# One core, a two-layer decoder trunk: the front of the recurrent layer with scaled evictions, six banks of low-rank products, and memory attention interleaved with the value strips

## The reference, cut to what matters

```python
proj = hn @ rwkv_w_in[j]
prev = jnp.pad(proj, ((0, 0), (1, 0), (0, 0)))[:, :-1]
xs = proj + (prev - proj) * mu                     # token shift
w = -jax.nn.softplus(-(w0 + jnp.tanh(wl) @ w2)) - 0.5
a = jax.nn.sigmoid(a0 + al @ a2)
g = jax.nn.sigmoid(gl) @ g2
kk = (k * k_k); kk = kk * rsqrt(max(sum(kk * kk), 1e-24))   # per head
k = k * (1.0 + (a - 1.0) * k_a)
bonus = sum(r * k * r_k) * v                       # per head
...
s = einsum('bshd,bmhd->bhsm', q, mem_k) * HEAD_DIM ** -0.5
p = softmax(s); mo = einsum('bhsm,bmhd->bshd', p, mem_v)
mix = concatenate([prim, mo]) @ w_out[i]
```

## Time and profile before

| | |
|---|---|
| median of 3 runs | 791.8 us (790.52 to 792.34) |
| the profiled execution's own time | 790.41 us |
| its span, first to last instruction | 788.7 us, mean granted clock 0.974 |
| PE busy | 736.8 us (93%) |
| DVE / ACT / POOL busy | 489.3 (62%) / 405.6 (51%) / 97.8 us (12%) |
| front of layer 1, first turned strip to first chunk matmul | 382.6 to 483.5 us |

### The profile page before, as it was taken

How to read it: one execution, slowest core, us unless ns; L and a number is a source line. 1 busy time by engine, 2 the same in 40 slices (tenths; PEclk the granted TensorE clock), 3 DMA queues, 4 the chain that set the end, 5 groups by cost and what they waited for, 6 DMA issues and landing times.

```text
span 788.7 us, 15563 instructions
## 1 busy us (share of the span) xinstructions
PE 736.8 (93%) x6725; PEld 641.1 (81%) x6725; DVE 489.3 (62%) x707; ACT 405.6 (51%) x641; POOL 97.8 (12%) x148
## 2 busy tenths in 40 slices
PE   3999998999999999999798788999899999999996
PEld 3879966788888888888787677999888888888885
DVE  4787776647766656444776995333557766566522
ACT  6654766548554555335865423333237645555311
POOL 4020076500000000000701004700000000000000
PEclk9999989999999999999979898999999999999998
DMA  8846710036565655565713430000026656565511
GB/s 299 298 143 207 256 46 1 2 114 229 166 198 175 198 176 197 180 209 161 227 53 111 158 106 3 4 5 4 3 82 223 203 165 207 164 211 166 209 54 54
DMA packets 78278, 111.73 MB, mean 142 GB/s; under 512 B 2124, under 2 KB 64738, under 8 KB 78210
## 3 DMA queue, kind: packets, MB, share of 16 engines
q1 hardware_dynamic: 77090, 107.67, 41.4%
q0 software_dynamic: 976, 3.04, 1.2%
q10 hardware_dynamic: 144, 0.04, 0.0%
HBM read 109.68 MB, written 1.05 MB: 140 GB/s over the span
## 4 chain that ended last, share of the span: by engine, by line
PE 77%; DVE 13%; ACT 6%; issue 2%; DMA 1%; POOL 1%; SPq 0%; DVEq 0%; ACTq 0%; POOLq 0%
PE ps L968 19%; PE ps L681 10%; PE ps L1109 10%; PE ps L682 10%; PE ps L683 10%; PE ps L970 10%; DVE w_lo L1706 3%; ACT w_hi L1276 2%; PE ps L813 2%; PE ps L839 2%; PE ps L790 1%; DVE x_hi_lo L1926 1%; DMA w_raw<-w_mem_kv 1%; DVE row_max L1786 1%; ACT scores L1342 1%
## 5 line engine op out<-in xcount | busy, mean ns | idle before, releaser
L1706 DVE TENSOR_TENSOR w_lo<-w_raw,w_hi 128x2048 fp32r<-128x2048 f32 (+2 forms) x101 | 227.4, 2263 | 91.4 <-ACT w_hi L1276 91.3
L968 PE MATMUL ps<-x_hi_lo,w_hi 128*128 128x512 f32 x640 | 226.5, 399 | 0.0
L1276 ACT ACTIVATE w_hi<-w_raw 128x2048 fp32r<-128x2048 f32 (+2 forms) x101 | 189.1, 1890 | 43.7 <-PE ps L683 42.9
L970 PE MATMUL ps<-x_hi_lo,w_lo 128*128 128x256 f32 x640 | 179.8, 281 | 0.0
L968 PEld LDWEIGHTS ps<-x_hi_lo,w_hi 128*128 128x128 f32 x640 | 120.3, 188 | 29.9
L970 PEld LDWEIGHTS ps<-x_hi_lo,w_lo 128*128 128x128 f32 x640 | 120.9, 189 | 0.0
L681 PE MATMUL ps<-w_hi,x_hi_lo 128*128 128x512 f32 (+3 forms) x240 | 82.7, 345 | 3.5 <-DVE x_hi_lo L1926 3.0
L683 PE MATMUL ps<-w_hi,x_hi_lo 128*128 128x512 f32 (+3 forms) x240 | 81.0, 337 | 0.0
L682 PE MATMUL ps<-w_lo,x_hi_lo 128*128 128x512 f32 (+3 forms) x240 | 81.0, 337 | 0.0
L681 PE MATMUL ps<-w_hi,hidden_hi 128*128 128x512 f32 x176 | 68.6, 390 | 0.0
L682 PE MATMUL ps<-w_lo,hidden_hi 128*128 128x512 f32 x176 | 68.5, 389 | 0.0
(11 more groups left out here) (365 smaller groups left out, 1122.5 us busy)
## 6 DMA issues: line engine op xcount, KB each, us to landing
w_raw<-w_ffn_in SPq DMA_DIRECT2D x44, 1024.0 KB, 5.1
w_raw<-w_ffn_out SPq DMA_DIRECT2D x22, 1024.0 KB, 4.9
w_raw<-rwkv_w_in SPq DMA_DIRECT2D x11, 1024.0 KB, 5.5
w_raw<-w_out SPq DMA_DIRECT2D x8, 1024.0 KB, 5.1
w_raw<-nsa_w_in SPq DMA_DIRECT2D x6, 1024.0 KB, 14.7
w_raw<-w_mem_kv SPq DMA_DIRECT2D x2, 1024.0 KB, 8.5
w_raw<-nsa_cmp_k_w SPq DMA_DIRECT2D x2, 1024.0 KB, 5.6
w_raw<-nsa_cmp_v_w SPq DMA_DIRECT2D x2, 1024.0 KB, 5.6
```

Source lines behind the costliest of these rows:

```text
L968: pe.matmul(psum[:, bank + j, :], kt_of(w_hi, i, k)[:, c], xx[:, k, :, :].rearrange("p c n -> p (c n)"), start=k == 0, stop=False)
L970: ins = pe.matmul(psum[:, bank + j, 0:SEQ], kt_of(w_lo, i, k)[:, c], xh[:, k, :], start=False, stop=k == KD - 1)
L1276: act.activation(w_hi[:, i % SPL, 0:size(i)], raw[:, i % RAW, 0:size(i)], ACT.Copy).then_inc(hi_done, 1)
L1706: dve.tensor_tensor(w_lo[:, i % RAW, 0:size(i)], raw[:, i % RAW, 0:size(i)], w_hi[:, i % SPL, 0:size(i)], ALU.subtract).then_inc(lo_done, 1)
```

## The change

The **token shift** becomes two evictions and one sum. ACT writes mu * strip into `shift_in` and (1 - mu) * strip straight into the destination, in four instructions of 128x256 with a per-partition scale where one copy of 128x512 stood; DVE adds the two in one instruction. The column 1 - mu (and 1 - k_a) is made once in `cols_m` by two small DVE instructions in layer 0. The **low-rank products** use six banks (0, 1, 2 for z and 3, 6, 7 for a), so that no pair waits for an eviction; PE no longer waits for the gate's sigmoid ahead of them, strip 3 comes ahead of the gate products, and ACT takes all three z before the three a and the gate's sigmoid after them. The factor 1 + (a - 1) * k_a goes from DVE to ACT, and the squares of `kk` from POOL to ACT. The **memory query** strip moves ahead of the value strips (`MQ` = 7), and the steps of the memory attention are put between and inside the strips 8, 9 and 10 (`feature_strip` gets a `between` after its first half), with the maxima, exponentials and copies put between the splits and strips of ACT and DVE. The turned probabilities go to bank 6, all values to bank 7, from which one ACT and one DVE instruction make the high and low part; only the last chunk waits for them. The products with exp(sums) move from q = 6 to q = 7 on DVE.

```diff
-RWKV_ORDER = [9, 3, 4, 5, 0, 1, 2, 6, 7, 8, 10]
+RWKV_ORDER = [9, 3, 4, 5, 0, 1, 2, 10, 6, 7, 8]
+MQ = RWKV_ORDER.index(10)
...
+        colM = put("one_minus_mu_ka", [P, 26])
...
-        pT1 = at(o_x, "probsT_1", [P, 2, 2, 2, P])
+        pT1 = at(o_cs, "probsT_1", [P, 2, 2, 2, P])
...
+        def strip_dst(q):
+            f0 = 2 * RWKV_ORDER[q]
+            dst = wg if q == 0 else (rT, k_T, vT)[f0 // FT]
+            j0 = 0 if q == 0 else f0 % FT
+            return f0, [dst[:, j0 + i, :] for i in range(2)], dst[:, j0:j0 + 2, :]
...
-            pool.wait_ge(kk_ok, 1)
-            pool.tensor_tensor(eP_sq[:], kkT[:], kkT[:], ALU.mult).then_inc(sq_ok, 1)
...
+            def lora_pair(j, bank, rows, src, done):
+                for i in range(2):
+                    f = 2 * j + i
+                    ins = pe.matmul(psum[:, bank, i * SEQ:(i + 1) * SEQ], lora[rows, f * P:(f + 1) * P], src, start=True, stop=True)
+                ins.then_inc(done, 1)
+            def memory_step(s):
+                if s < NMEM:
+                    scores(1, s)
+                if 0 <= s - LAG_T < NMEM:
+                    probs_turn(1, s - LAG_T)
+                if 0 <= s - LAG_V < NMEM:
+                    values(1, s - LAG_V)
             tok_strips(1, first["rwkv"])
             strip_turns(0)
             strip(2)
             strip_turns(1)
             pe.wait_ge(in_lora, 48)
-            pe.wait_ge(fm_out, 2)
+            pe.wait_ge(a_lo, N_UNITS - NMEM)
+            pe.wait_ge(shifted, 1)
+            pe.wait_ge(l_act, 1)
+            for j in range(FT // 2):
+                lora_pair(j, j, slice(0, LORA), wg[0:LORA, 0, :], z_mm)
+            for j in range(FT // 2):
+                if j == 1:
+                    pe.wait_ge(fm_out, 2)
+                lora_pair(j, (3, 6, 7)[j], slice(LORA, P), wg[LORA:P, 0, :], a_mm)
+            strip(3)
             pe.wait_ge(l_act, 2)
...
+            pe.wait_ge(z_ev, 3)
             for j in range(FT // 2):
...
-            strip(3)
             strip(4)
             pe.wait_ge(sq_ok, 1)
...
-            for q in range(5, 9):
+            for q in range(5, MQ + 1):
                 strip(q)
+            pe.wait_ge(ss_ev, 3)
+            pe.wait_ge(a_ev, 3)
+            def first_scores():
+                pe.wait_ge(fm_out, MQ + 1)
+                memory_step(0)
+            strip(MQ + 1, first_scores)
+            memory_step(1)
+            strip(MQ + 2, lambda: memory_step(2))
+            memory_step(3)
+            strip(MQ + 3, lambda: memory_step(4))
+            memory_step(5)
             pe.wait_ge(rk_ok, 1)
-            pe.wait_ge(ss_ev, 3)
+            pe.wait_ge(a_exp, N_UNITS)
...
-            strip(9)
-            strip(10)
-            pe.wait_ge(bo_ev, 3)
-            pe.wait_ge(fm_out, 11)
-            attention(1)
+            memory_step(6)
+            memory_step(7)
...
-            pe.wait_ge(a_lo, N_UNITS)
+            pe.wait_ge(fm_out, MQ + 4)
+            pe.wait_ge(bo_ev, 3)
             pe.wait_ge(ar_ok, 1)
             pe.wait_ge(bk_ok, 1)
             pe.wait_ge(shifted, 10)
             pe.wait_ge(rwkv_ok, 7)
             for c in range(NCH):
+                if c == NCH - 1:
+                    pe.wait_ge(a_lo, N_UNITS - NMEM + 1)
...
-                if q >= 2:
-                    act.wait_ge(shifted, q - 1)
-                act.activation(shb[q % 2][:, :, 1:SEQ + 1], src, ACT.Copy).then_inc(fm_out, 1)
+                    act.wait_ge(vec_ev, 2)
+                n = shift_no(q)
+                if n >= 2:
+                    act.wait_ge(shifted, n - 1)
+                f0, dst, _ = strip_dst(q)
+                for i in range(2):
+                    act.activation(shb[n % 2][:, i, 1:SEQ + 1], src[:, i, :], ACT.Copy, scale=col(B_MU, f0 + i))
+                    ins = act.activation(dst[i], src[:, i, :], ACT.Copy, scale=colM[:, f0 + i:f0 + i + 1])
+                ins.then_inc(fm_out, 1)
...
+                if q == MQ + 1:
+                    exps(1, 0)
+                if q == MQ + 2:
+                    exps(1, 2)
+                if q == MQ + 3:
+                    probs_out(1, 0)
                 strip_out(q)
+                if q == MQ + 1:
+                    exps(1, 1)
+                if q == MQ + 2:
+                    exps(1, 3)
                 if q == 0:
                     act.wait_ge(shifted, 1)
                     act.activation(wg[0:LORA, 0, :], wg[0:LORA, 0, :], ACT.Tanh).then_inc(l_act, 1)
-                    act.activation(wg[:, 1, :], wg[:, 1, :], ACT.Sigmoid).then_inc(l_act, 1)
                 if q == 1:
                     for j in range(FT // 2):
                         act.wait_ge(z_mm, j + 1)
...
                         ins.then_inc(z_ev, 1)
+                    for j in range(FT // 2):
...
                         ins.then_inc(a_ev, 1)
+                    act.activation(wg[:, 1, :], wg[:, 1, :], ACT.Sigmoid).then_inc(l_act, 1)
                 if q == 2:
+                    act.wait_ge(a_ev, 3)
+                    for f in range(FT):
+                        ins = act.activation(vT[:, f, :], aT[:, f, :], ACT.Identity, bias=colM[:, 20 + f:21 + f], scale=col(B_KA, f))
+                    ins.then_inc(l_act, 1)
...
                 if q == 3:
+                    act.wait_ge(kk_ok, 1)
+                    act.activation(eP_sq[:], kkT[:], ACT.Square).then_inc(sq_ok, 1)
...
-            attention(1)
+            probs_out(1, 2)
             split_to(first["rwkv"] + 11 + 3 + AHEAD)
+            act.wait_ge(used, first["rwkv"] + 11)
+            act.wait_ge(a_pv, N_UNITS)
+            act.activation(xh[:, FT:KD, :], psum[:, 7, :].rearrange("p (f n) -> p f n", n=SEQ), ACT.Copy).then_inc(a_hi, 1)
...
-                f0 = 2 * RWKV_ORDER[q]
-                dst = wg if q == 0 else (rT, k_T, vT)[f0 // FT]
-                j0 = 0 if q == 0 else f0 % FT
-                link(dve.tensor_tensor(dst[:, j0:j0 + 2, :], shb[q % 2][:, :, 0:SEQ], shb[q % 2][:, :, 1:SEQ + 1], ALU.subtract))
-                for i in range(2):
-                    ins = dve.scalar_tensor_tensor(dst[:, j0 + i, :], dst[:, j0 + i, :], col(B_MU, f0 + i),
-                                                   shb[q % 2][:, i, 1:SEQ + 1], ALU.mult, ALU.add)
-                ins.then_inc(shifted, 1)
+                _, _, dst = strip_dst(q)
+                dve.tensor_tensor(dst, dst, shb[shift_no(q) % 2][:, :, 0:SEQ], ALU.add).then_inc(shifted, 1)
...
-            for q in range(10):
+            for q in range(11):
+                if q in (0, 3):
+                    shift(q)
+                if q == 3:
+                    dve.wait_ge(shifted, 4)
+                    dve.wait_ge(rwkv_ok, 7)
+                    for f in range(FT):
+                        ins = dve.tensor_scalar(kkT[:, f, :], k_T[:, f, :], col(B_KK, f), None, ALU.mult)
+                    ins.then_inc(kk_ok, 1)
                 split_to(first["rwkv"] + q + 3 + AHEAD)
-                shift(q)
+                if q == MQ:
+                    en = eN[:].rearrange("p f t n -> p (f t n)")
+                    dve.tensor_tensor(aT[:].rearrange(flat), aT[:].rearrange(flat), en, ALU.mult)
+                    dve.tensor_tensor(k_T[:].rearrange(flat), k_T[:].rearrange(flat), en, ALU.mult).then_inc(bk_ok, 1)
+                if q == MQ + 1:
+                    maxima(1, 0)
+                if q == MQ + 2:
+                    maxima(1, 2)
+                    factors(1, 1)
+                if q == MQ + 3:
+                    factors(1, 3)
+                    probs_out(1, 1)
+                if q not in (0, 3, MQ):
+                    shift(q)
+                if q == MQ + 1:
+                    maxima(1, 1)
+                    factors(1, 0)
+                if q == MQ + 2:
+                    maxima(1, 3)
+                    factors(1, 2)
...
                 if q == 3:
-                    dve.wait_ge(shifted, 4)
-                    dve.wait_ge(rwkv_ok, 7)
-                    for f in range(FT):
-                        ins = dve.tensor_scalar(kkT[:, f, :], k_T[:, f, :], col(B_KK, f), None, ALU.mult)
-                    ins.then_inc(kk_ok, 1)
-                    dve.wait_ge(a_ev, 3)
-                    for f in range(FT):
-                        ins = dve.tensor_scalar(vT[:, f, :], aT[:, f, :], -1.0, col(B_KA, f), ALU.add, ALU.mult)
-                    link(ins)
-                    link(dve.scalar_tensor_tensor(k_T[:].rearrange(flat), vT[:].rearrange(flat), 1.0, k_T[:].rearrange(flat),
-                                                  ALU.add, ALU.mult))
+                    dve.wait_ge(l_act, 3)
+                    dve.wait_ge(kk_ok, 1)
+                    link(dve.tensor_tensor(k_T[:].rearrange(flat), vT[:].rearrange(flat), k_T[:].rearrange(flat), ALU.mult))
...
-                    en = eN[:].rearrange("p f t n -> p (f t n)")
-                    dve.tensor_tensor(aT[:].rearrange(flat), aT[:].rearrange(flat), en, ALU.mult)
```

(6 more changed lines are left out.)

56 lines of the change are left out of this document (26 added, 30 removed).

## The result

The changed kernel takes 794.45 us in the median of 20 runs (790.86 to 795.79), the kernel before in the same comparison 790.44 us (785.16 to 792.80): a ratio of 1.0051, 95% interval 1.0034 to 1.0068, so 4.0 us slower, with 2.7 to 5.4 in the interval. A second comparison gave 794.26 against 789.62 us, 1.0070 (1.0045 to 1.0095). The forecast was no change, 791.7 us, in a range that holds the measured time.

What follows compares the result with a forecast made beforehand. PE alone bounds the chunk phase, so only its start, 483.50 us, counts. The 5.6 us won up to the bonus factor are given back behind it (38.8 against 33.3 us): 791.7 us against 791.8, range 787.0 to 796.0.

Steps and rivals of the forecast that it cites:

- Step 1: Layer 1 front: ACT evicts strip 1, loads a table, does six z sigmoids; scans start at 394.8 us, 4.7 earlier.
- rival E: Low-rank products: still at half clock, ACT gets z 1.5 us later; 793 us, chance 5%.
- Step 2: Behind the z sigmoids: ACT works without a gap for 12.9 us, to 407.8; DVE idles 4 us.
- Step 3: Up to Ln: DVE's shift, kk, split and sums, ACT's square and exponentials; Ln starts at 422.6 us, 3.7 earlier.
- rival D: ACT dearer: 0.48 per eviction on seven strips (+2.8) or two table loads (+2.6); 794.5 us, chance 13%.
- Step 5: DVE without a gap through the bonus factor: 15.9 us, ending at 444.6 against 450.23; 5.6 us won so far.
- Step 6: DVE behind the bonus factor: split, two products, split, first maximum, to 453.4 us.
- Step 7: Memory attention: ACT and DVE alternate, 17.05 us and seven hand-overs, first probability copy done at 471.1 us.
- Step 8: PE, having waited for the first probability copy, does 6.2 us of work, two thirds at half clock, to 477.3.
- rival C: Half clock after PE's wait for the probability copy lasts into bonus products and first chunks; 795 us, chance 22%.
- Rival B: Steps right but lighter: PE at full clock after its wait (-2.1), overlapping hand-overs (-1.5); 788.1 us, chance 23%.
- Rival A: Memory attention hidden whole, DVE never waiting behind the bonus factor; chunks start at 467, time 775 us, chance 4%.

Runs made afterwards that it cites:

- early_copy: The changed kernel with ACT's copy of unit 0's probabilities moved ahead of the exponentials of unit 2: 791.62 us.
- after_pad: The changed kernel with 128 bytes left free behind its new tile of 26 columns: 791.38 us, ratio to before 1.0015.
- lora_only: The kernel before with only the low-rank products in the new form (six banks, z first, gate behind): 784.61 us, ratio 0.9940.
- the best version: The changed kernel with 128 bytes free, first maximum right behind the bonus factor, last pieces' splits deferred, probability copy earlier: 773.53 us, ratio to before 0.9787.

## Why the prediction was wrong, and where it was right

Its timeline held. Times of the changed kernel with 0.62 added, against the forecast:

- Step 1, scans at 394.8: 394.7. That z would come at half clock (rival E) falls: the products' clock is 1.00, where in before, with a wait between the pairs, it was 0.55. The windows from the first low-rank product to the last, after and before:

```profile
388.72:393.41 4.69, 4.69 (x26) 3.90 (x25) 2.07 (x2) 4.55 (x10) 1.87 (x2) 1.00 0.74 224
391.32:399.25 7.93, 6.88 (x25) 4.53 (x25) 3.22 (x4) 3.76 (x10) 0.00 (x0) 0.55 0.30 106
```

- Step 2, ACT through to 407.8, DVE idle 4: 408.0 and 4.49.
- Step 3, Ln at 422.6: 422.8. No table load was added for Identity or Square (there are five from 380 to 430 us, as in before), and an eviction with pointer scale costs 0.36 (398.12, 398.48, 398.83, 399.19): rival D falls. The factor's six took 2.95 us (402.50 - 399.55), against 2.2 taken and 2.8 as the other end: with bias and scale both by pointer one costs 0.49. Step 2's work on ACT took 13.55 us (393.87 to 407.42) against 12.9 forecast, and the excess is this factor's; it began 0.3 us earlier than forecast, so the end held.
- Step 5, bonus factor ends at 444.6: 444.9. Step 6, first maximum done at 453.4: 453.6 (452.80 + 0.17 + 0.62).
- Step 7, first probability copy done at 471.1: 471.0, with ACT idle 14.79 us ahead of the first exponentials.
- Step 8, 477.3: PE idle 6.66 us, then half clock as forecast, 6.5 us from 470.49 to 477.00, so 477.6. (That PE waited for the copy, which the row doesn't say, is what early_copy showed.) The window from 470 to 474 us shows it, and the next ones how it ends:

```profile
470.00:474.00 4.00, 3.51 (x18) 2.88 (x19) 2.90 (x3) 0.39 (x1) 1.60 (x2) 0.50 0.02 4
474.00:478.00 4.00, 4.00 (x32) 3.66 (x31) 0.00 (x0) 0.99 (x3) 0.23 (x1) 0.81 0.00 0
478.00:482.84 4.84, 4.39 (x33) 3.48 (x33) 3.27 (x5) 2.86 (x4) 0.00 (x0) 1.00 0.65 217
```

  The clock is at 1.00 before the chunks begin, so rival C falls: it doesn't reach into them.
- Step 9, chunks at 483.4: 483.5.

One wait the prediction didn't name: PE also stands 8.02 us ahead of the scores of unit 2, until ACT has done the exponentials of unit 0, and the clock from 449 to 457 us is 0.50.

```profile
454.08 1.23 PE L802 MATMUL ps<-mem_kT,mem_qT 64*128 64x256 f32 x4 [8.02 <-ACT scores L1373]
```

Steps 6 and 7 still took their time, since DVE and ACT were the late engines there.

The step that failed is the sum around them. The prediction says that the change is worth what it moves the start of the chunk phase "and nothing else", and prices the new columns by their two instructions, at 0.1 us. The columns also take 128 bytes of the allocation, and the 264 matmuls in each of the two down projections pay 6.7 ns each for where the hidden layer then lies: 3.4 to 3.5 us by the rows, 2.1 to 3.4 in the medians of four pairs. That is the cause of most of the 4.0 and 4.6 us. What is left, the stage in its order with the tiles in place, is after_pad's ratio of 1.0015 (0.9999 to 1.0032), which is the forecast of no change, or at most slightly above it. Rival B, a lighter alternation, has nothing left: each of its steps took the forecast time. Rival A, in the order as forecast, didn't come either. None of the rivals had the place of the tiles; the range held the time by rival C's and D's prices, not by its cause.

Two readings behind the right sum were off. First, steps 1 to 5 give the 5.6 us as one sum of shift, low-rank products and factor, and don't say which carries it. The trace confirms the sum (5.3 to 5.9 at the bonus factor), but lora_only shows 4.2 to 4.8 of it from the banks and the order of z alone; shift and factor, the larger part of the edit, give 1.1 there, and in the medians nothing that can be told with the rest unchanged. DVE's 0.9 us a strip was right and ACT's 1.0 us a strip was right, and up to Ln they lie on the same path. Second, the prediction gave rival A 4% and said that half of it could not be found in the queues, with splits ahead of the waits. That was true of the kernel as changed. With two splits out of the stretch, the others and the two products moved, and the first maximum taken early, the chunks start 17.2 us sooner than in the changed kernel: what stood against A was less the waits in order than what stood between them. That this is close to A's 16.5 is in part luck: A's sum has all four of DVE's splits (8.9 us) and no waiting, the best version has two of them and DVE busy 16.6 of 21.2 us.
